# 32 instead of 16 tokens computed by gathered rows, and another split of the first product's row operations between VectorE and GpSimd

## What is computed

```python
def peer_ffn(h, w_pq, sub_keys, expert_u, expert_v):
    q = (h @ w_pq).reshape(B, S, PEER_HEADS, 2, PEER_DQ // 2)
    scores = jnp.einsum('bshpd,hpkd->bshpk', q, sub_keys)
    top_s, top_i = lax.top_k(scores, K)                      # K = 16, of 128 keys, for 8 heads
    cand_s = top_s[..., 0, :, None] + top_s[..., 1, None, :]
    cand_i = top_i[..., 0, :, None] * NK + top_i[..., 1, None, :]
    best_s, best_pos = lax.top_k(cand_s.reshape(B, S, PEER_HEADS, K * K), K)
    expert_idx = jnp.take_along_axis(cand_i, best_pos, axis=-1)
    gate = jax.nn.softmax(best_s, axis=-1)
    u = jnp.take(expert_u, expert_idx, axis=0)
    a = jnp.einsum('cd,chkd->chk', h, u)
    w = gate * jax.nn.gelu(a, approximate=False)
    return jnp.einsum('chk,chkd->cd', w, jnp.take(expert_v, expert_idx, axis=0))
```

## Time and profile before

| | us |
|---|---|
| median of three runs | 2776.13 (2773.47 to 2776.21) |
| the profiled execution, its own time | 2772.15 |
| its span in the trace | 2770.4 |
| PE busy | 2693.1 (97%) |
| DVE busy | 2127.9 (77%) |
| ACT busy | 1381.1 (50%) |
| POOL busy | 382.7 (14%) |

### The profile page before, as it was taken

How to read it: one execution, slowest core, us unless ns; L and a number is a source line. 1 busy time by engine, 2 the same in 40 slices (tenths; PEclk the granted TensorE clock), 3 DMA queues, 4 the chain that set the end, 5 groups by cost and what they waited for, 6 DMA issues and landing times.

```text
span 2770.4 us, 39894 instructions
## 1 busy us (share of the span) xinstructions
PE 2693.1 (97%) x16254; PEld 2321.3 (84%) x16254; DVE 2127.9 (77%) x3176; ACT 1381.1 (50%) x1632; POOL 382.7 (14%) x294
## 2 busy tenths in 40 slices
PE   7999999999999999999999999999999999999998
PEld 6778888788888888998888888897889988788887
DVE  7787887775555579989978777646699989888776
ACT  4645446554455455554444344464555554434443
POOL 0210002000023001122102012040011222002121
PEclk8999999999999999999999999999999999999999
DMA  8757876466553355555456588644555655456785
GB/s 312 268 198 296 313 257 225 155 213 197 190 199 129 135 190 191 205 198 170 166 183 212 185 290 295 225 150 139 165 180 197 209 182 176 149 198 218 258 289 185
DMA packets 86470, 574.34 MB, mean 207 GB/s; under 512 B 9840, under 2 KB 10352, under 8 KB 23056
## 3 DMA queue, kind: packets, MB, share of 16 engines
q1 hardware_dynamic: 75888, 534.86, 55.1%
q0 software_dynamic: 10400, 36.93, 3.8%
HBM read 563.32 MB, written 8.44 MB: 206 GB/s over the span
## 4 chain that ended last, share of the span: by engine, by line
PE 84%; DVE 8%; ACT 3%; issue 3%; DMA 1%; POOL 1%; SPq 0%; POOLq 0%; DVEq 0%; ACTq 0%
PE banks L492 22%; PE banks L499 11%; PE banks L590 11%; PE banks L592 10%; PE banks L600 10%; DVE wlo L1610 3%; PE banks L564 2%; PE banks L566 2%; PE banks L575 2%; ACT whi L1095 2%; PE banks L1030 2%; PE banks L534 1%; PE banks L536 1%; PE banks L546 1%; PE banks L630 1%
## 5 line engine op out<-in xcount | busy, mean ns | idle before, releaser
L1095 ACT ACTIVATE whi<-raw 128x2048 fp32r<-128x2048 f32 x438 | 839.7, 1917 | 962.6 <-issue 761.7
L1610 DVE TENSOR_TENSOR wlo<-raw,whi 128x2048 fp32r<-128x2048 f32 x422 | 977.0, 2315 | 240.6 <-ACT whi L1095 239.8
L492 PE MATMUL banks<-ht,whi 128*128 128x480 f32 (+1 forms) x2848 | 675.1, 387 | 5.9 <-DVE big L1708 3.4
L492 PEld LDWEIGHTS banks<-ht,whi 128*128 128x128 f32 x2848 | 524.0, 190 | 88.9 <-issue 3.6
L590 PE MATMUL banks<-whi,ht 128*128 128x512 f32 x1152 | 454.5, 395 | 10.4 <-DVE ht L1698 10.4
L592 PE MATMUL banks<-whi,ht 128*128 128x512 f32 x1152 | 449.8, 390 | 0.0
L499 PEld LDWEIGHTS banks<-ht,wlo 128*128 128x128 f32 x2848 | 351.7, 190 | 11.4
L499 PE MATMUL banks<-ht,wlo 128*128 128x240 f32 (+1 forms) x2848 | 354.0, 277 | 0.0
L600 PE MATMUL banks<-wlo,ht 128*128 128x512 f32 x1152 | 288.8, 390 | 2.1 <-DVE wlo L1610 2.1
L590 PEld LDWEIGHTS banks<-whi,ht 128*128 128x128 f32 x1152 | 216.9, 188 | 56.5 <-issue 12.1
L600 PEld LDWEIGHTS banks<-wlo,ht 128*128 128x128 f32 x1152 | 216.7, 188 | 47.9 <-DVE wlo L1610 3.0
(11 more groups left out here) (311 smaller groups left out, 3579.1 us busy)
## 6 DMA issues: line engine op xcount, KB each, us to landing
raw<-in_pu SPq DMA_DIRECT2D x128, 1024.0 KB, 4.9
raw<-in_pv SPq DMA_DIRECT2D x128, 1024.0 KB, 4.9
raw<-in_win SPq DMA_DIRECT2D x52, 1024.0 KB, 4.9
big<-in_wmod SPq DMA_DIRECT2D x28, 1024.0 KB, 7.1
raw<-in_wgate SPq DMA_DIRECT2D x22, 1024.0 KB, 6.4
raw<-in_wup SPq DMA_DIRECT2D x22, 1024.0 KB, 5.7
raw<-in_wdown SPq DMA_DIRECT2D x22, 1024.0 KB, 5.0
raw<-in_wmod SPq DMA_DIRECT2D x20, 1024.0 KB, 5.1
```

The lines of the kernel that those rows point to most:

```text
L492: m = e.matmul(wide(b + n, t), h[:, q, c[n]], x[:, q], start=q == 0, stop=False, skip_group_check=True)
L1095: e.activation(whi(j), slot[u][0], ACT.Copy).then_inc(*hi.mark(j))
L1610: e.tensor_tensor(wlo(j), slot[u][0], whi(j).bitcast(F32), ALU.subtract).then_inc(*lo.mark(j))
```

## The change

FEW goes from 16 to 32, so NT from 240 to 224 and the gate groups from 30 to 28. The gathered rows are 32 + 32 per layer, with eight buffers. The gate groups are new in odd units only, two or three at a time, and the last are due in unit 62. POOL makes the remainders of the 13 odd units 37 to 61 of the first product (before, of eight, every third unit). The table has one entry per head for units made between the heads' work, all empty here. `dots_due` puts 6 rows into units 10 to 25 of the second product and 26 into units 28 to 42; `adds_due` puts 32 into units 44 to 61. Buffers move, so that POOL may read the slots behind unit 5 of the second product.

```diff
--- before.py
+++ after.py
@@ -24,12 +24,12 @@
 UN = 2048
 NRAW = 3
 GATES = 36
-FEW = 16
+FEW = 32
 NT = 256 - FEW
 SUB = P // FEW
 NG = NT // 8
-RINGS = 4
-POOLED = (37, 40, 43, 46, 49, 52, 55, 58)
+RINGS = 8
+POOLED = (), (), (), (), (), (), (), (), tuple(range(37, 62, 2))
 NSP = 2
 NEG = -1e30
 LOW = -3.0e38
@@ -200,7 +200,7 @@
     HI = at("whi", 24576, NSP * UN, F32R)
     LO = at("wlo", 40960, NSP * UN, F32R)
     HT = Halves(at("ht", 57344, 2 * UN, F32R)[:, :])
-    OH = [[at(f"oh0{i}", 73728 + 4 * (29696 + 1024 * i), 2048, F16) for i in range(3)],
+    OH = [[at(f"oh0{i}", 73728 + 4 * (28672 + 1024 * i), 2048, F16) for i in range(3)],
           [at("oh1a", 65536, 2048, F16), at("oh1b", 65536 + 4096, 2048, F16)]]
     AG = at("big", 73728, 32768, F32)
     HID = Halves(at("hid", 73728 + 4 * 25600, 2048, F32R)[:, :])
@@ -282,9 +282,10 @@
     QT, KY, SC = 13312, 17408, 19456
     TV, TIU, TIF, BV, BP, AF, BF = (23552 + 512 * i for i in range(7))
     E1, E2, RP, II, SS = 27136, 29184, 31232, 31744, 32512
-    HREP, ACC, ROWS_OF, PICK = 2048, 3072, 4096, 4096 + 1024 * RINGS
+    HREP, ACC, PICK = 28672, 29696, 2048
+    ROWS_OF = 30720, 31744, *range(2560, 8704, 1024)
     SLOTS, IDU, IDV, DOTS, IDF, IDC = (PICK + 128 + FEW * i for i in (0, 3, 4, 5, 6, 7))
-    DENSE = -(-(IDC + FEW) // (2 * NT)) - 1
+    DENSE, *DENSE_ROWS = (-(-x // (2 * NT)) - 1 for x in (ROWS_OF[2], *(y + 1024 for y in ROWS_OF[2:])))
     def gcols(l, i):
         return COLS[:, l * 64 + 24 + i * 8:l * 64 + 32 + i * 8]
 
@@ -352,7 +353,7 @@
     scratch = nc.dram_tensor("xs", [2 * P, D], F32, kind="Internal").ap()
     few_rows = [nc.dram_tensor(f"fewr{l}", [P, D], F32, kind="Internal").ap() for l in range(DEPTH)]
     few_ids = [nc.dram_tensor(f"fewi{l}", [FEW, 3 * P], F32, kind="Internal").ap() for l in range(DEPTH)]
-    pooled = {first["pu", l] + u for l in range(DEPTH) for u in POOLED}
+    pooled = {first["pu", l] + u for l in range(DEPTH) for us in POOLED for u in us}
 
     def low_at(k):
         return (p_lo if k in pooled else lo).at(k)
@@ -392,16 +393,18 @@
         return first["ffn", l] + (4 + 3 * i if i < 10 else 32)
 
     def pace(u):
-        return 2 if u % 16 == 1 else 1
+        return 3 if u % 12 == 1 else 2 if u % 2 else 0
 
     def second_pace(v):
         return 2 if v % 2 == 0 else 0
 
     def dots_due(v):
-        return 1 if 31 <= v < 47 else 0
+        if v < 28:
+            return 1 if v % 3 == 1 and v >= 10 else 0
+        return 0 if v > 42 else 1 if v % 4 == 0 else 2
 
     def adds_due(v):
-        return 0 if v < 48 or v > 60 else 2 if v % 4 == 1 else 1
+        return 0 if v < 44 or v > 61 else 1 if v % 4 == 0 and v > 44 else 2
 
     def region(on, l, u):
         if u < 12:
@@ -414,7 +417,7 @@
         if 2 * NT * (u + 1) > SC:
             on.wait_ge(*took_v.at(("top", l, 1)))
             on.wait_ge(*d_ids.at(l))
-        if u >= 61:
+        if u >= 63:
             on.wait_ge(*took_v.at(("hot", l, 0, NG - 1)))
             on.wait_ge(*gated.at((l, 0, NG - 1)))
 
@@ -1039,11 +1042,11 @@
                         for i in range(3):
                             m = e.transpose(bank[b][:, i * 128:(i + 1) * 128], ag(II + (t * 3 + i) * 128, 128), IDN)
                         m.then_inc(*turned.mark(("top", l, t)))
-                if u == 61:
+                if u == 63:
                     while plan.left():
                         for g in plan.step(2)[0]:
                             gate(0, g)
-                due = plan.step(pace(u))[0] if GATES < u < 61 else []
+                due = plan.step(pace(u))[0] if GATES < u < 63 else []
 
                 def between():
                     for g in due:
@@ -1567,7 +1570,7 @@
                 k = take()
                 if v:
                     split_weights(v + 1)
-                if v == 48:
+                if v == 43:
                     on.wait_ge(*few.at((l, "dot", FEW - 1)))
                     e.activation(ag(DOTS, FEW), ag(DOTS, FEW), ACT.Gelu).then_inc(*a_soft.mark(("few", l)))
             last_h[0] = k
@@ -2315,7 +2318,7 @@
                 if u == GATES:
                     slots_turned(l, 0)
                     slots_turned(l, 1)
-                if GATES < u < 61:
+                if GATES < u < 63:
                     gate_step(l, 0, *plan.step(pace(u)))
                 if u < GATES - 2:
                     some(2.2)
@@ -2327,7 +2330,7 @@
             def row(m):
                 r = m % RINGS
                 on.wait_ge(*d_row[r].at((l, m)))
-                return ag(ROWS_OF + 1024 * r, 1024)
+                return ag(ROWS_OF[r], 1024)
 
             def dot(n):
                 x = row(n)
@@ -2602,14 +2605,21 @@
             on.wait_ge(*d_gain.at(l))
             e.tensor_tensor(ag(HREP, 1024), ag(HREP, 1024), ag(ACC, 1024), ALU.mult).then_inc(*p_rep.mark(l))
 
+        def remainder(j):
+            on.wait_ge(*hi.at(j))
+            on.wait_ge(*unit.at(j - NSP))
+            e.tensor_tensor(wlo(j), slot[place_of[j]][0], whi(j).bitcast(F32), ALU.subtract).then_inc(*p_lo.mark(j))
+
         def gathered(l, m):
             r, n = m % RINGS, m % FEW
+            if 2 <= m < RINGS:
+                on.wait_ge(*part_lo.at(("w", l, DENSE_ROWS[m - 2])))
             if m >= RINGS:
                 x = m - RINGS
                 on.wait_ge(*few.at((l, "dot", x) if x < FEW else (l, "added", x - FEW)))
             table, at_ = ((a["urow"], IDU), (a["vrow"], IDV))[m // FEW]
             on.wait_ge(*p_ids.at((l, "v")))
-            e.indirect_dma_start(ag(ROWS_OF + 1024 * r, 1024), None, table,
+            e.indirect_dma_start(ag(ROWS_OF[r], 1024), None, table,
                                  bass.IndirectOffsetOnAxis(ag(at_ + n, 1).bitcast(U32), 0)).then_inc(*d_row[r].mark((l, m)))
 
         def peer(l):
@@ -2625,16 +2635,16 @@
                         eh = ag(E2 + h % 2 * 1024 + w * 512 + t * 256, 256).rearrange("p (k a) -> p k a", k=16)
                         tf = ag(TIF + t * 256 + (2 * h + w) * 16, 16).unsqueeze(1).broadcast_to([P, 16, 16])
                         e.tensor_tensor(eh, eh, tf, ALU.mult).then_inc(*p_mul.mark((l, "pick", h, w)))
+                if h < 7:
+                    for u in POOLED[h]:
+                        remainder(first["pu", l] + u)
             on.wait_ge(*top.at((l, "final")))
             for w in range(3):
                 o = II + 384 + w * P
                 e.dma_start(few_ids[l].rearrange("t (s w n) -> t w s n", s=SUB, w=3)[:, w],
                             AG[P - FEW:P, o:o + P].rearrange("t (s n) -> t s n", s=SUB)).then_inc(*d_ids.mark(l))
-            for u in POOLED:
-                j = first["pu", l] + u
-                on.wait_ge(*hi.at(j))
-                on.wait_ge(*unit.at(j - NSP))
-                e.tensor_tensor(wlo(j), slot[place_of[j]][0], whi(j).bitcast(F32), ALU.subtract).then_inc(*p_lo.mark(j))
+            for u in POOLED[8]:
+                remainder(first["pu", l] + u)
             on.wait_ge(*row_free.at((l, 63, 3)))
             e.memset(HT.both.rearrange("p (q n) -> p q n", n=256)[:, 0:8, NT:256].bitcast(F32), 0.0).then_inc(*p_zero.mark(l))
             on.wait_ge(*d_ids.at(l))
```

## The result

The changed kernel takes **2726.7 us** (median of 4 runs, 2726.0 to 2731.4) against 2775.0 us for the kernel before in the same comparison: a ratio of 0.983, with a 95% interval of 0.981 to 0.985. Forecast were 2853 us and "slower", with 0.76. The time is that of the first rival, to the microsecond, and lies inside the wide range only because that rival was let into it.

The account below looks back on a forecast made before the run. TensorE (PE), with 84% of the chain, was taken as the bound. Terms -27 + 2 - 21 + 91 + 2 + 34 = +81 us on 2772.2 gave 2853 us; own range 2815 to 2877, widened to 2724 to 2877 for the first rival.

Parts of the forecast that it names:

- the first rival: Gate stage: DVE keeps its row together, or POOL arrives 0.5 us later; no stall, -46 us, 2726 us; chance 0.20.
- The shorter matmuls: First product, 240 to 224 tokens: high matmuls 13 ns shorter, 0.21 us a unit, 27 us saved; low ones 0.
- What gives some back: Units 4 to 36 of the first product: DVE, nearly full, returns 1 us per layer, 2 us in all.
- The gates: Units 37 to 62: 28 groups inside units and no burst, 10.4 us less per layer, 21 us in all.
- The wait that I expect: Even units: POOL's remainder blocks DVE's one-hots, PE waits 3.8 us before the second group, 24 times; 91 us.
- rows 7: Trace of the kernel before: once per layer POOL's multiply got between two back-to-back DVE operations, the second taking 2.89 us.
- The clock: PE idle during each expected stall loses granted clock: 1.4 us per stall, 24 stalls, 34 us; bounds 0 to 2.3 each.
- The row work: Second product: 32 + 32 gathered rows per layer hidden behind PE, DMA at 354 GB/s; charged 0, up to +12 us.
- The sum: Whole kernel: -27 + 2 - 21 + 91 + 2 + 34 = +81 us on 2772.2, giving 2853 us.
- third groups: Gate steps of three groups instead of two: about 1 us more PE wait per layer, 2 us in all.
- The rule I leaned on: DVE and POOL: the shared pair is held for one whole instruction, issue order decides; used against the rival without a stall.

Follow-up runs that it names:

- the kernel with the gap: Changed kernel plus a one-column memset between the second and third one-hot operation of each step's last gate group; 2856.6 us, ratio 1.029 to the kernel before.
- the bench: Test programs without the network: a GpSimd operation released into rows of back-to-back VectorE operations, 33 tests, then 34 more; no kernel time.
- the memset ahead: Changed kernel plus a one-column memset ahead of the one-hot operations of each odd unit, before POOL's remainder arrives; 2833.7 us, ratio 1.023 to the kernel before.

## Why the prediction was wrong

*The shorter matmuls.* Right. 217 ns became 203 (the median distance between starts), and a plain unit went from 5.271 to 5.046 us, 0.225 against my 0.21; the low ones gave nothing, as I took it, and the run with 192 columns shows a floor of 111 ns. The Trainium skill (TensorE: Matmul & The Clock Gate, LDWEIGHTS) gives 107 ns for such a load; as an estimate from that, the step to 224 columns could have given 5 ns each; the traces show 1 (112 and 111).

*What gives some back.* Right. 36 units less 0.225 each are 8.1 us, measured 6.6 and 6.4 a layer: about 1.6 came back, where I charged 1.

*The gates.* Right. I forecast 10.4 us a layer and 27 x 0.21 = 5.7 for the shorter units, 16.1 together; measured are 16.5 and 15.7.

*The wait that I expect.* **This is the step that failed**, and in it one sentence: "The waiting POOL operation went between two that stood back to back. So POOL gets in behind the second operation (T + 5.7) and keeps DVE out for about 4.5 us." The observation was right, the "so" wasn't: in the changed kernel POOL waited through DVE's row to its end, 24 times of 24. In rows 7 POOL's operation arrived during the first one-hot behind a remainder at whose end another POOL operation had just had the pair; here the row was seven operations old, counted from the remainder. All else around it held: the arrival (T + 5.5), the blocking, and, in the kernel with the gap, PE's wait (87.2/25 = 3.5 us against 3.8). Of +91 us came 0; PE waited for one-hots in four places, 1.8 us in all.

*The clock.* The term fell with the wait. Where the wait was made, 43 us over 25 stalls are 1.7 each; I took 1.4, between 0 and 2.3.

*The row work.* Right at 0: the second product lost nothing. DMA gave 361 GB/s in those 100 us against my 354, at a share of 0.97, so there was little left. The gathers took 1.9 to 2.0 us on POOL on average, where I had taken 0.94, and the second product lost nothing by it.

*The sum.* -27 + 2 - 21 = -46 was rival 1; between the two profiled executions, from which the forecast counted, measured are 2726.0 - 2772.15 = -46.2 (-48.3 between the medians). Its sum leaves out the 2 us for third groups, which measured 1.8; a gate group took (6.09 - 5.05)/2 = 0.52 us instead of 0.56, 2.2 us less in 56 groups. That these two cancel is luck. The rival was right about what happened, and wrong about its margin: "it decides at half a microsecond" is not so. POOL came at the time I said. What decided is the number of the operation during which it came, and the kernel stands on the 7th, the first that keeps POOL out, with one exception in another kernel. I gave it 0.20, and called one case in each layer evidence against it; a row that shows an effect once doesn't say under which conditions it is absent.

*The rule I leaned on.* The Trainium skill (SBUF — State Buffer, Who interferes with whom) has DVE or GpSimd hold the shared pair for one instruction, whoever issues first, and says that issue order decides. For a young row the runs agree (0.36 us from arrival to entry, then 4.7 us of blocking), and its list of who takes the pair agrees with what counts here. For a row of seven or more they don't: a GpSimd operation that had waited for 2.7 us (4.2 in the bench) was passed by six DVE operations and more. Here the measurement decides.

## What to carry to other kernels

- When an engine waits for a shared resource, look not only for a case where it got in, but at what the holder had done before: number the holder's operations since its last gap. On VectorE a cheap operation of the wrong kind (a memset, 0.06 us) in a row of one-hots cost 107 to 130 us; a copy in its place cost 1.
- An offload that frees an engine with room to spare buys nothing (2725.9 without it, 2726.7 with it). Remove it before tuning its phase, above all where the gain hangs on one operation.
- A half of a change can be worth nothing or 12 us, by what the other half is: the new gate order beside the old set of units, and without any. A table with both halves in and out shows it; one undone part doesn't.

## What the runs showed that I had not expected

- A GpSimd operation that comes during one of VectorE's first six SBUF operations (two operands, or a copy) since a wait, a memset or GpSimd's last turn gets in at the next boundary. From the seventh on it waits until the row ends. So it was in all 67 bench tests of such rows. In the kernels it nearly was: with the memset ahead 6 of 23 arrivals on the sixth stayed out, and 1 of the 83 on the seventh or above got in. It was the same for operations of 0.34 us and 2.2 us, for a 2048 subtract, a 1024 multiply and a tensor_scalar of 32 columns on GpSimd, which so waited 4.2 us to do 0.3 us of work.
- Operations that read PSUM neither count nor break the count, but let a waiting GpSimd operation in. Why seven, and why the edge isn't sharp in the kernel, the runs don't say.
